# Seven block products in place of eight for 8 of the 22 k tiles of two output pairs of the down projection

## What is computed

```python
up = rmsnorm(x, g2) @ w_up                  # 1024 -> 5632
conv = c_b + c_w[0]*pad[:, 0:S] + ...       # causal, width 3
a, gval = jnp.split(conv, 2, axis=-1)
x = x + (jax.nn.silu(a) * gval) @ w_down    # 2816 -> 1024: the down projection
y = rmsnorm(x, g_final)
```

## Time and profile before

| | us |
|---|---|
| median of 3 runs | 907.29 |
| the profiled execution's own time | 907.64 |
| its span, first to last instruction | 905.8 |
| down projection, first matmul of tile 0 to last of tile 7 | 769.87 to 897.4 |
| PE busy | 897.4 |
| DVE busy / ACT busy | 553.7 / 374.0 |

### The profile page before, as it was taken

How to read it: one execution, slowest core, us unless ns; L and a number is a source line. 1 busy time by engine, 2 the same in 40 slices (tenths; PEclk the granted TensorE clock), 3 DMA queues, 4 the chain that set the end, 5 groups by cost and what they waited for, 6 DMA issues and landing times.

```text
span 905.8 us, 19411 instructions
## 1 busy us (share of the span) xinstructions
PE 897.4 (99%) x7378; PEld 892.8 (99%) x7378; DVE 553.7 (61%) x863; ACT 374.0 (41%) x582; POOL 134.1 (15%) x181
## 2 busy tenths in 40 slices
PE   9999999999999999999999999999999999999997
PEld 9999999999999999999999999999999999999997
DVE  7895774443885444397756787777777777433234
ACT  7545434535863333243432344444444444322232
POOL 0672000011541111000006600000000000000001
PEclk9999999999999999999999999999999999999998
DMA  6332262243962222222253222222222222323332
GB/s 211 118 117 94 70 220 85 71 124 137 323 235 71 80 83 70 93 93 87 98 210 102 89 76 92 91 93 93 93 93 93 93 93 87 98 85 94 98 85 95
DMA packets 31345, 100.30 MB, mean 111 GB/s; under 512 B 4652, under 2 KB 7244, under 8 KB 31048
## 3 DMA queue, kind: packets, MB, share of 16 engines
q1 hardware_dynamic: 29256, 92.96, 30.7%
q0 software_dynamic: 1328, 5.72, 2.0%
q10 hardware_dynamic: 720, 1.04, 0.4%
HBM read 92.37 MB, written 7.35 MB: 110 GB/s over the span
## 4 chain that ended last, share of the span: by engine, by line
PE 89%; issue 3%; POOLq 3%; DMA 2%; DVE 1%; POOL 1%; ACT 0%; DVEq 0%; SPq 0%; ACTq 0%
PE out L1698 84%; PE trp L1698 2%; POOLq L1676 2%; PE aux L1698 1%; POOLq L1674 1%; DMA raw_pair<-in_w_slots 1%; PE trp L1730 1%; DMA cwb<-in_conv_wb 1%; PE aux L1887 0%; ACT whi L525 0%; POOL y L1689 0%; DVE wlo L970 0%; POOL out_conv_old L1660 0%; DVEq L1517 0%; POOLq L86 0%
## 5 line engine op out<-in xcount | busy, mean ns | idle before, releaser
L970 DVE TENSOR_TENSOR wlo<-raw_pair,whi 128x1024 fp32r<-128x1024 f32 (+1 forms) x139 | 177.0, 1274 | 194.3 <-ACT whi L525 194.0
L525 ACT ACTIVATE whi<-raw_pair 128x1024 fp32r<-128x1024 f32 (+3 forms) x156 | 155.2, 997 | 253.3 <-PE out L1698 241.6
L1698 PE MATMUL out<-xh,whi 128*128 128x260 f32 x728 | 152.9, 288 | 0.4 <-ACT gtmp L525 0.4
L1698 PE MATMUL out<-xh,wlo 128*128 128x260 f32 x728 | 148.6, 283 | 0.0
L1698 PE MATMUL out<-xl,whi 128*128 128x260 f32 x728 | 148.3, 283 | 0.0
L1698 PE MATMUL out<-x2h,wlo 128*128 128x260 f32 x704 | 142.0, 283 | 0.0
L1698 PE MATMUL out<-x2h,whi 128*128 128x260 f32 x704 | 141.9, 283 | 0.0
L1698 PE MATMUL out<-x2l,whi 128*128 128x260 f32 x704 | 141.8, 283 | 0.0
L1698 PEld LDWEIGHTS out<-xh,whi 128*128 128x128 f32 x728 | 113.4, 189 | 1.1 <-ACT gtmp L525 0.6
L1698 PEld LDWEIGHTS out<-xh,wlo 128*128 128x128 f32 x728 | 113.0, 188 | 0.0
L1698 PEld LDWEIGHTS out<-xl,whi 128*128 128x128 f32 x728 | 112.9, 188 | 0.0
(11 more groups left out here) (310 smaller groups left out, 1475.9 us busy)
## 6 DMA issues: line engine op xcount, KB each, us to landing
raw_pair<-in_w_slots SPq DMA_DIRECT2D x123, 512.0 KB, 3.3
raw_pair<-in_w_dn SPq DMA_DIRECT2D x16, 448.0 KB, 3.3
c_ring<-in_C_state SPq DMA_DIRECT2D x8, 512.0 KB, 4.5
row<-scratch SPq DMA_DIRECT2D x8, 512.0 KB, 6.0
out_C_sample<-c_ring SPq DMA_DIRECT2D x8, 512.0 KB, 4.0
raw_pair<-in_w_dn SPq DMA_DIRECT2D x8, 512.0 KB, 3.6
xres<-in_x_all POOLq DMA_DIRECT2D x1, 2080.0 KB, 8.8
x<-in_x_all SPq DMA_DIRECT2D x5, 260.0 KB, 6.8
```

The lines of the kernel that those rows point to most:

```text
L525: return act.activation(out, in_, func, **kw_)
L970: TT(wlo[p][:, 0:width], raw[p][:, 0:width], whi[p][:, 0:width].bitcast(F32), ALU.subtract)\
L1698: return pe.matmul(*a, **k)
```

## The change

For output tile pairs (2,3) and (4,5), the first slot of each tile (k tiles 0 to 7) is no longer multiplied tile by tile. The 8 k tiles by 2 output tiles by 2 token halves are seen as a 2x2 by 2x2 block product and made with 7 block products of 12 matmuls (Strassen's method in Winograd's form). Three products lead into PSUM banks in which the other 14 k tiles then go on adding; four go to PSUM banks of their own (`trp`, `aux`) and are added to `x1` by DVE.

- Activation combinations (`dtf`, `dth`, `dtl`, four blocks of 128x1040): four `down_sum`, four `down_difference`, four high parts on ACT, four `down_combination_low` on DVE. They are made once, during tiles 0 and 1.
- Per pair: four weight sums, seven factors high and low (128x512) in place of two slots of 128x1024, seven additions of 260 columns on DVE, one copy on ACT.
- The loops of the down projection are written out on SP, ACT, DVE and PE. The scaling by the gain (`xg`) of tiles 0 to 5, formerly after each tile, comes in one batch on ACT after slot S_DN+20 is split, since `dth` lies where `xg` is.
- The order on DVE around the change, as the diff has it:

```diff
+            def down_weight_sums(pr):
+                dve.wait_ge(s_nc, 2 * FT)
+                for n in pr.n[0:2]:
+                    dve.wait_ge(w_loaded[n.c % 2], n.half(1) * 16)
+                TT(dsum[:, 0, :], pr.a21, pr.a22, ALU.add).then_inc(s_sw, 1)
+                dve.drain()
+                TT(dsum[:, 1, :], dsum[:, 0, :], pr.a11, ALU.subtract).then_inc(s_sw, 1)
+                TT(dsum[:, 2, :], pr.a11, pr.a21, ALU.subtract).then_inc(s_sw, 1)
+                dve.drain()
+                TT(dsum[:, 3, :], pr.a12, dsum[:, 1, :], ALU.subtract).then_inc(s_sw, 1)
+            def down_first_factors_low(pr):
+                down_weight_sums(pr)
+                factor_low(pr, 0)
+                factor_low(pr, 1)
+            def down_pair(pr):       
+                factor_low(pr, 2)
+                factor_low(pr, 3)
+                factor_low(pr, 4)
+                dn_sum(n[0].plus(-1), j - 1)
+                dn_squares(j - 1)
+                factor_low(pr, 5)
+                factor_low(pr, 6)
...
+                low(n[3], width(2))
+                low(n[4], width(1))
+                dn_sum(n[3], j)
+                dn_squares(j)
+                low(n[5], width(2))
+            def down_pair(pr):
+                act.wait_ge(done, n[1]())
+                factor_hi(pr, 2)
+                factor_hi(pr, 3)
+                act.wait_ge(s_pd, 6 * q + 1)
+                factor_hi(pr, 4)
+                A(dtmp[:, 1, :], pr.p1).then_inc(s_dc, 1)
+                act.wait_ge(s_pd, 6 * q + 2)
+                factor_hi(pr, 5)
+                dn_square(pr.j - 1)
...
+                split(n[3], width(2))
+                split(n[4], width(1))
+                split(n[5], width(2))
+                dn_square(pr.j)
+            def down_pair(pr):
+                if pr.i > 1:
+                    pe.wait_ge(s_dr, pr.i - 1)
+                product(pr, 0, pr.p1, *down_quarter(0, 0)).then_inc(s_pd, 1)
+                pe.wait_ge(s_tl, 8)
+                product(pr, 1, pr.p6, *down_combination(2)).then_inc(s_pd, 1)
+                product(pr, 2, pr.p5, *down_combination(0)).then_inc(s_pd, 1)
+                product(pr, 3, pr.p7, *down_combination(1)).then_inc(s_pd, 1)
+                pe.wait_ge(evac[S_DN % 2], At(S_DN + pr.j).half(1))
+                product(pr, 4, banks[0][:, 0, 0:HALF], *down_quarter(1, 0), last=False).then_inc(s_pd, 1)
+                product(pr, 5, banks[0][:, 1, 0:HALF], *down_quarter(1, 1), last=False).then_inc(s_pd, 1)
+                pe.wait_ge(evac[(S_DN + 1) % 2], At(S_DN + pr.j + 1).half(1))
+                product(pr, 6, banks[1][:, 0, 0:HALF], *down_combination(3), last=False).then_inc(done, 2)
+                for s in range(2, 6):
...
             dn_pair(0, True)
-            with pe.Fori(1, KT // 2 - 1) as i:
-                dn_pair(i)
+            for pr in pairs_d:
+                down_pair(pr)
             dn_pair(3, count=3)
             last_tile()
```

More of the change, by code:

```diff
@@ L142, in hybrid_layer @@
         LAST = (DN_CUTS[3] - DN_CUTS[2]) * P
+        dth = at("dth", [P, 4, KT // 2, HALF], 0, F32R)
+        dtl = at("dtl", [P, 4, KT // 2, HALF], XB, F32R)
+        dtf = at("dtf", [P, 4, KT // 2, HALF], XB)
+        dsum = at("dsum", [P, 4, HW], F0 + 6688)
+        dtmp = at("dtmp", [P, 2, HALF], F0 + 14880)
         whi_last = at("whi_last", [P, LAST], F0 + 6688, F32R)
@@ L281, in place, with __init__ @@
                 return w[self.t0 if f % 4 < 2 else self.t1][:, (f % 2) * HW:(f % 2 + 1) * HW]
+        class DownPair(Pair):
+            def __init__(self, i):
+                self.q = (KT - PLAIN) // 2 + i - 1
+                self.i, self.j = i, 2 * i
+                self.n = [At(S_DN + 6 * i + t) for t in range(6)]
+                self.t0, self.t1 = self.n[0].c % 2, self.n[1].c % 2
+                self.p1, self.p6 = (trp[t][:, :, :].rearrange("p a b -> p (a b)")[:, 0:HALF] for t in range(2))
+                self.p5, self.p7 = (aux[:, t, 0:HALF] for t in range(2))
+                r0, r1 = raw[self.t0], raw[self.t1]
+                self.a11, self.a12, self.a21, self.a22 = r0[:, 0:HW], r0[:, HW:], r1[:, 0:HW], r1[:, HW:]
+                self.factor = (self.a11, dsum[:, 1, :], dsum[:, 0, :], dsum[:, 2, :], self.a12, dsum[:, 3, :], self.a22)
+        pairs_d = [DownPair(i) for i in (1, 2)]
         pairs_w = [Pair(q) for q in range((KT - PLAIN) // 2)]
@@ L385, in hybrid_layer @@
         s_gs = sem("gate_sigmoids")
+        s_dr = sem("down_products_read")
+        s_dc = sem("down_product_copied")
         s_nh = sem("branch_half_hi")
@@ L502, in _, with down_weights, down_width, load_down @@
             load_slots(S_WO, S_DN)
-            with sp.Fori(0, KT // 2) as i:
-                for s in range(6):
-                    a, b = DN_CUTS[s % 3], DN_CUTS[s % 3 + 1]
-                    load(At(S_DN + s, i, 6), ins["w_dn"][i * 2 + s // 3, :, a * P:b * P], (b - a) * P)
+            def down_weights(j, q):
+                return ins["w_dn"][j, :, DN_CUTS[q] * P:DN_CUTS[q + 1] * P]
+            def down_width(q):
+                return (DN_CUTS[q + 1] - DN_CUTS[q]) * P
+            def load_down(i):
+                for s in range(6):
+                    load(At(S_DN + 6 * i + s), down_weights(2 * i + s // 3, s % 3), down_width(s % 3))
+            load_down(0)
+            for pr in pairs_d:
+                load(pr.n[0], down_weights(pr.j, 0))
+                load(pr.n[1], down_weights(pr.j + 1, 0))
+                sp.wait_ge(s_pl, 7 * pr.q + 5)
+                sp.dma_start(raw[pr.t0][:, 0:down_width(1)], down_weights(pr.j, 1)).then_inc(w_loaded[pr.t0], 16)
+                sp.wait_ge(s_pl, 7 * pr.q + 7)
+                sp.dma_start(raw[pr.t1][:, 0:down_width(2)], down_weights(pr.j, 2)).then_inc(w_loaded[pr.t1], 16)
+                load(pr.n[4], down_weights(pr.j + 1, 1), down_width(1))
+                load(pr.n[5], down_weights(pr.j + 1, 2), down_width(2))
+            load_down(3)
             def store_y(a, j0, j1):
@@ L903, in split_last, with width, dn_square @@
                 A(whi_last[:, :], raw[n.c % 2][:, 0:LAST]).then_inc(s_wh, 1)
[L905 to L916, removed]
+            def width(s):
+                return (DN_CUTS[s % 3 + 1] - DN_CUTS[s % 3]) * P
+            def dn_square(j):
                 act.wait_ge(s_x2f, j + 1)
@@ L919, in dn_result, with dn_gained, down_combination_hi @@
                 A(sqa[:, :], x1[:, j, :], ACT.Square).then_inc(s_sqf, 1)
[L920 to L925, removed]
+            def dn_gained(j):
+                A(xg[:, j, :], x1[:, j, :], scale=gains[:, 3, j:j + 1])
+            def down_combination_hi(r):
+                act.wait_ge(s_bt, 4 + r + 1)
+                A(dth[:, r, :, :], dtf[:, r, :, :]).then_inc(s_th, 1)
@@ new lines, in down_first_factors_hi @@
+            def down_first_factors_hi(pr):
+                act.wait_ge(w_loaded[pr.t0], pr.n[0].half(1) * 16)
+                act.wait_ge(done, pr.n[0]())
+                factor_hi(pr, 0)
+                act.wait_ge(s_sw, 4 * pr.q + 4)
+                factor_hi(pr, 1)
+            def down_pair(pr):
+                q, n = pr.q, pr.n
+                act.wait_ge(done, n[1]())
[7 more added lines that the diff above has]
+                dn_square(pr.j - 1)
+                act.wait_ge(s_pd, 6 * q + 3)
+                factor_hi(pr, 6)
+                act.wait_ge(w_loaded[pr.t0], n[2].half(1) * 16)
+                act.wait_ge(s_pd, 6 * q + 5)
+                A(whi[pr.t0][:, 0:HW], raw[pr.t0][:, 0:HW]).then_inc(s_nh, 1)
+                act.wait_ge(s_pd, 6 * q + 6)
+                A(whi[pr.t0][:, HW:width(1)], raw[pr.t0][:, HW:width(1)]).then_inc(w_hi, 3)
+                split(n[3], width(2))
+                split(n[4], width(1))
+                split(n[5], width(2))
+                dn_square(pr.j)
@@ new lines, in _ @@
+            for s in range(3):
+                split(At(S_DN + s + 2), width(s + 2))
+            dn_square(0)
+            split(At(S_DN + 5), width(5))
+            down_combination_hi(0)
+            down_combination_hi(1)
+            down_combination_hi(2)
+            down_combination_hi(3)
+            down_first_factors_hi(pairs_d[0])
+            down_pair(pairs_d[0])
+            down_first_factors_hi(pairs_d[1])
+            down_pair(pairs_d[1])
+            split(At(S_DN + 18), width(0))
@@ L926, in _ @@
+            split(At(S_DN + 19), width(1))
+            dn_square(5)
+            split(At(S_DN + 20), width(2))
+            for j in range(KT - 2):
+                dn_gained(j)
+            split(At(S_DN + 21), width(0))
+            split(At(S_DN + 22), width(1))
+            split_last()
+            dn_square(6)
+            dn_gained(6)
             table_of_sqrt()
@@ L1504, in low_last, with width, dn_sum, dn_squares @@
                     .then_inc(s_wl, 1)
[L1506 to L1516, removed]
+            def width(s):
+                return (DN_CUTS[s % 3 + 1] - DN_CUTS[s % 3]) * P
```

(99 more changed lines are left out.)

3 lines of the change are left out of this document (added).

## The result

| | before | changed |
|---|---|---|
| median, 20 runs each | 907.31 us | 909.16 us |
| lowest and highest | 906.69, 909.78 | 907.78, 911.15 |
| the profiled execution, its span | 907.64, 905.8 | 909.3, 907.6 |

The ratio of the changed kernel to the one before is 1.0016, with a 95% interval of 1.0010 to 1.0022: some 1.5 us slower, just inside the 0.2% band. The medians lie 1.85 us apart (0.20%), the means of the 20 runs 1.34 us (0.15%); the ratio, which is made from all runs, lies between them and is what the text goes by. So it is slower, by about as much as the band is wide.

What follows compares the result with a forecast made beforehand. PE was taken to bound the kernel, so only fewer matmuls gain time. The terms -2.88 + 2.93 + 0.99 = +1.04 us on the profiled 907.64, against the median 907.29, gave 908.3 us; range 906.7 to 909.9.

Steps and rivals of the forecast that it cites:

- the forecast's own range: 907.5 to 908.9 us, the range for the summed forecast of 908.3 us; with D it had chance 0.77.
- B: Slower: PE's granted clock falls to half in the first wait, +1.5 us to 909.8, or +10 if longer; chance 0.11.
- C: Slower: the load before the second pair lands late, 4.9 us, 1.3 more than the forecast's term: 909.6; chance 0.05.
- grant 1.00 through the pause: Expected in the profile after: PE's granted clock stays full through the 2.6 to 3.1 us wait before the first pair.
- if the grant falls: A named sign of the prediction being wrong: PE's granted clock drops from its full level.
- The saving: In the down projection's two pairs, 24 fewer matmuls at 0.1202 us take 2.88 us off PE's path.
- The first wait: Before the first pair's product 0, PE waits 2.93 us, 801.60 to 804.53, for DVE's low of the first factor.
- The second wait: Before the second pair, PE waits 0.99 us; its weight sums need a load issued only after slot n[5]'s low.
- rival A: Faster: DVE is in time before both pairs, waits as short as branch a's 0.2 us, 904.8 us; chance 0.07.
- Inside a pair: Within each pair, factors, additions and loads are ready before PE wants them; no wait, margins of over 0.8 us.
- Batch of scalings: Six scalings on ACT after slot S_DN+20's split, 4 us in all, with 4.8 us of cover behind: no PE wait.
- D: One wait before a pair is smaller, the first by up to 0.5 us; down to 906.8; shares 0.77 with the forecast.

Runs made afterwards that it cites:

- e1_order: The changed kernel with its steps before the first pair reordered so the first factor's inputs come first, same work; 905.72 us, 0.9981 of the kernel before.
- e3_second: The changed kernel with the low of slot n[5] put ahead of the square's addition on DVE; 908.18 us, 1.0006 of the kernel before.
- e4_both: The changed kernel with the edits of e1_order and e3_second together; 904.73 us, 0.9969 of the kernel before.
- e0_as_changed: The changed kernel measured again without edits, in another batch on another chip; 909.11 us, 1.0022 of the kernel before.
- e5_fill11: The changed kernel with 11 unused matmuls added between tile 1 and the wait for factor 0; 907.92 us, 1.0005 of the kernel before.

## Why the prediction was right, and where not

The range, 906.7 to 909.9, held the time, and "within 0.2%" is what the ratio gives (1.0016). Both held narrowly. The median, 909.16, lies above the forecast's own range of 907.5 to 908.9, and only the part of the range that was there for B and C takes it in; the repeat came out at 1.0022. The two waits were right in place, cause and about in size. The clock was not: "grant 1.00 through the pause" failed in all three profiles with that pause, and "if the grant falls" was one of the signs of being wrong. The forecast itself, 908.3, fits the six executions whose mean grant stayed up (908.2 on average); the others are rival B, which I gave 0.11.

- **The saving, 2.88 us.** Right. The second pair took 30.29 us for 252 matmuls, 30.28 expected, and the kernel without waits came out 2.7 below before with 0.2 left. The estimate of 2.66 from the Trainium skill's spacing ("TensorE: Matmul & The Clock Gate", section "Wait — 56ns, not 53.3ns?") can't be told from it by a time, but the spacing of 0.120 in the trace rules it out.
- **The first wait, 2.93.** Measured 2.80. The chain held step by step: from the start of slot 5's low to product 0 I had 11.73 us, the trace has 11.62 (792.39 to 804.01). e1_order shows that the order of DVE's steps makes it.
- **The second wait, 0.99.** Measured 0.72. The term that was off is the load: the first sum came 3.52 after the low's end, 3.84 expected. SP issued 0.03 after the low's end (829.44 against 829.41), not 0.17, and the landing took 3.4 us, not 3.6. e3_second shows the cause.
- **Branch a as a measure.** The prediction put both waits of the earlier trace rows into the block products of branch a and took 0.2 us as what the chain before a second pair cost there. That was misread. The 0.2 belongs to the first matmul of the stage behind branch a, which waits for an ordinary low (L970), not for a factor's (L1343):

```profile
445.67 0.41 PE L1698 MATMUL out<-hah,wlo 128*128 128x260 f32 x2
...
468.69 0.51 PE L1698 MATMUL out<-mh,whi 128*128 128x260 f32 x2 [0.22 <-DVE wlo L970]
```

The second pair of branch a started at 445.98, where the spacing gives 445.91: 0.07 us late. The sum did not use the 0.2; only rival A's price did.

- **Inside a pair.** No wait, as worked out; the only delay in any variant is the 0.17 us before product 5 in e1_order and e4_both.
- **Batch of scalings.** Hidden: it ran from 873.72, six in 3.81 us, and ACT then still sat idle for 0.38 before the next split. A seventh would have been late for it.
- **The clock.** This is the term that my sum lacked. I had rival B as a possibility of 0.11 with +1.5 us if the lower level lasts as long as the pause. The profile shows 1.52 lost, but that the price agrees is luck: the lower level lasted 3.4 us, not 2.9, and a matmul at half took 0.217, not 0.24. I held it unlikely since full streams stand on both sides; they do not protect the clock. The Trainium skill (same page, section "HAM oscillation — how this bites in real kernels") says that the burst after a long gap starts cold, which no row showed before. In e0_as_changed it did: the grant fell before product 0. In the other two profiles it fell 0.4 us (changed kernel) and 1.3 us (e3_second) into the burst, so the cold stretch need not begin with it.
- **Rival A** (DVE in time) fell: the waits sum to 3.5 us, and it needed under 1.1. In branch a the combinations were long done.
- **Rival C** (a late load) fell: the load landed in 3.4 us, not 4.9.
- **D** (smaller waits) came true in small part: 0.13 us less at the first, 0.27 at the second.

What stays open: what gaps between 1.3 and 2.6 us do, which were not tried, and what decides in which executions, and at what moment, the clock falls.

## What to carry to other kernels

When PE is the bound and the saving is small, look at what the other engines must finish before the first instruction of the new form, and in what order they take it: here the 2.9 us of 24 saved matmuls were lost mainly because combinations wanted by product 1 and later stood ahead of the factor wanted by product 0. Put the inputs of the first consumer first, and whatever a buffer's next load waits for ahead of bookkeeping like squares. And count a PE gap like this one, 2.6 us, at more than its length: fill it, shorten it, or add what the clock takes.

## What was not expected of the hardware

- An idle gap of 2.6 us of PE between dense streams took the granted clock to half for 3.4 us, three times in three profiles (changed kernel, its repeat, e3_second), and cost 1.5 us beside the wait in the profile, 1.2 us between the medians of e0_as_changed and e5_fill11. In the profiles a gap of 1.3 us (e5_fill11) and gaps of 0.6 to 0.9 before the second pair didn't.
- The fall can come before the stream goes on (803.6 against a start at 803.85, e0_as_changed) or more than 1 us after (804.7 against 803.39, e3_second).
- Eleven useless matmuls in the gap made the kernel 1.2 us faster than the same wait left idle (907.92 beside 909.11). Twenty-two, in the other batch, gave 908.00 and a ratio of 1.0006.
